# Two edits to a two-network float32 forward pass: attention statistics and head steps, and the recurrent mixer's taps, decays and padding units

## The chip, the core and the metric

The kernel runs on one core of one Trainium2 chip. The metric is the device time of one execution in microseconds. A core has TensorE (PE, matrix products into PSUM), VectorE (DVE), ScalarE (ACT), GpSimd (POOL) and SyncE (SP, which here only issues transfers). The engines run their own instruction streams in order and wait for one another on semaphores.

## The reference

The kernel computes two small networks in a row on 256 tokens with model width 1024, all in float32. Only the parts around the change are shown; feed-forward and convolution blocks stand between them.

```python
# first network, layer 0: 8 MLA heads and 8 forgetting ("fox") heads, 16 meta tokens in front
q = (rms_norm(c_q, g_cq) @ w_uq).reshape(b, l, MLA_HEADS, MLA_QK)
kv = (rms_norm(c_kv, g_ckv) @ w_ukv).reshape(b, l, MLA_HEADS, MLA_NOPE + MLA_V)
q = rope_tail(rms_norm(q, g_q_mla), cos, sin)
k = rope_tail(rms_norm(k, g_k_mla), cos, sin)
qf = rms_norm(fq.reshape(b, l, FOX_HEADS, FOX_DIM), g_q_fox)
kf = rms_norm(fk.reshape(b, l, FOX_HEADS, FOX_DIM), g_k_fox)
# both groups: blocked causal softmax attention (fox with cumulative log forget gates), then @ w_out

# second network, layer 1: the recurrent mixer
def mixer_b(h, w_in, conv_w, conv_b, w_a, b_a, w_x, b_x, lam, w_out):
    g, xb = jnp.split(h @ w_in, 2, axis=-1)
    g = jax.nn.gelu(g)
    xb = causal_dwconv(xb, conv_w, conv_b)          # 4 taps
    xh = xb.reshape(bsz, s, B_HEADS, B_HDIM)
    r = jax.nn.sigmoid(jnp.einsum("bshd,hde->bshe", xh, w_a) + b_a).reshape(bsz, s, B_WIDTH)
    i = jax.nn.sigmoid(jnp.einsum("bshd,hde->bshe", xh, w_x) + b_x).reshape(bsz, s, B_WIDTH)
    log_a = LRU_C * r * jax.nn.log_sigmoid(lam)
    a = jnp.exp(log_a)
    mult = jnp.sqrt(-jnp.expm1(2.0 * log_a))
    bterm = mult * (i * xb)
    _, hs = lax.associative_scan(_lin_rec_op, (a, bterm), axis=1)
    return (hs * g) @ w_out
```

## The kernel before

**Units.** Each float32 product is made of three products of float32r halves: weights hi with activations hi, weights hi with activations lo, weights lo with activations hi. The weights come in units of 8 (or 6) blocks of 128x128; a unit is 24 (or 18) matmuls on TensorE. SyncE fetches slabs of two units into `raw`, a ring of four slabs. For each unit ScalarE writes `whi` (`split_hi`, L361) and VectorE `wlo` (`split_lo`, L366), each into a ring of four. The splits run LA = 3 units ahead of the unit that the step works on: `ahead` in step j splits unit j+3, and `split_hi` waits until TensorE has left the unit four before.

**A phase's head.** The last steps of a phase split units 0, 1 and 2 of the next phase. Unit 3 is split in `act_root` and `dve_rstd`, ahead of the normalisation's root and reciprocal. That statistic is summed on GpSimd and multiplied out on TensorE (`pe_stats`, L447) after unit 1 of the new phase; ScalarE takes the root (L460) and VectorE the reciprocal (L467).

**Attention.** The first 18 units give tiles of 128 rows; ScalarE squares and copies the fox tiles, TensorE sums the squares by head (`fox_stats`), ScalarE and VectorE turn them into inverse norms, and `spread` (L911) spreads one over a pair of heads, into one of two PSUM banks that `fox_normed` (L1335) empties. The heads then run as a pipeline over 18 items (fox diagonal item, 8 fox heads, the first MLA head, the MLA diagonal item "D1" as item 10, 7 MLA heads). In step st TensorE does the scores of item st, the transposes (`turn`) of item st-2 and the values of item st-3; VectorE takes the maximum (`peak`) and the normalisation (`normal`), ScalarE the exponential (`exps`) and the copies (`turned`, `high`). The sums of squares of the MLA queries are products with 8 columns (`q_stats`, L952), seven for each of three parts, two passes each. `LATE` says in front of which steps the weights of the next phase are split.

**Recurrent mixer (`b_in`, 32 units, then `b_out`, 16 units of 6 blocks).** The order is written out by hand:

```python
B_ORDER = [("x", 0), ..., ("x", 5), ("r", 0), ("x", 6), ("x", 7), ("r", 1), ("x", 8), ("x", 9), ("r", 2),
           ("x", 10), ("x", 11), ("r", 3), ("g", 0), ("g", 1), ("g", 2), ("r", 4), ("g", 3), ("r", 5), ("g", 4)...]
```

An `x` unit gives one tile of the convolution's input, an `r` unit both gates of a pair of tiles, a `g` unit one gate tile. In step k VectorE splits unit k+3 (L366), scales tile k out of PSUM (L1611) and runs three taps of the tile before it (`taps`, L1597); behind an `r` step there is no tile waiting for its taps. GpSimd does the first tap with the bias (L2151) and, two steps behind, the lo half `hlo` (L2156) of what ScalarE wrote as `hhi` (L1954). It also multiplies the gate into the tile (L2147), squares the decays (L2138) and forms the scan's input (L2163). `r` unit f waits for `hlo` of tiles 2f and 2f+1. Tables such as `B_DECAY` and `B_MINUS` say in which step which tiles have their exponentials and tanh (L1960, L1962), the 1-a^2 (L1621), the root, the scan (L1626), the product with the gate (L1632) and the last halves (L1974, L1637). Units 30 and 31 of `b_in` are empty; of them one block is split, and TensorE skips them, adding 3 to `unit_done` at its last unit.

## Time and profile before

| | us |
|---|---|
| median of 3 runs | 1367.07 |
| lowest, highest of the three | 1361.7, 1375.7 |
| the profiled execution | 1372.0 |
| its span in the profile | 1370.3 |
| TensorE busy | 1333.2 (97%) |
| VectorE busy | 970.7 (71%) |
| ScalarE busy | 740.8 (54%) |
| GpSimd busy | 395.0 (29%) |

The page divides the span into 40 slices and gives the granted TensorE clock of each. The timeline gives for each group of instructions its start, its duration, and in brackets the idle time before it with what ended it. The windows view gives busy time by engine in a stretch.

### The profile page before, as it was taken

Reading aid. Unit: us, or ns where it says so; the run is one execution under the profiler, and the core shown is the slowest. Engines: PE = TensorE matmul, PEld = TensorE weight load, DVE = VectorE, ACT = ScalarE, POOL = GpSimd, SP = SyncE. Lnnn points to the kernel's source line nnn. Section 1 sums busy time; section 2 is a strip of 40 time slices with the busy share of each in tenths; the row PEclk is TensorE's granted clock in tenths of the full one; section 3 lists DMA queues with packets and bytes.
Section 4 is the critical chain, followed back from the end, with each engine's and each line's share of the span. In section 5 each row is a group of like instructions: output and inputs, shape, how many; then the busy total and the mean of one; then the engine's idle time right before and its main releaser. Section 6 shows DMA issues by size and latency. Waiting matters only on the chain. (4 is left out here: it accounts for less than half of the span.)

```text
span 1370.3 us, 28906 instructions
## 1 busy us (share of the span) xinstructions
PE 1333.2 (97%) x10820; PEld 1295.2 (95%) x10820; DVE 970.7 (71%) x1437; ACT 740.8 (54%) x1204; POOL 395.0 (29%) x406
## 2 busy tenths in 40 slices
PE   9999899999999999999999999999999899999996
PEld 8887599999999999999989999999999889999996
DVE  5856677665578777655655569998559798999854
ACT  5454655444444544444555547666455786766642
POOL 3621014320001233200445413333015541343310
PEclk9997999999999999999999999999999999999998
DMA  9430044555545555555544555554654445555451
GB/s 311 151 115 1 31 154 158 183 191 182 184 179 185 185 175 188 191 185 184 193 146 154 185 185 178 188 185 139 207 208 152 156 161 209 185 184 184 149 198 54
DMA packets 35372, 230.53 MB, mean 168 GB/s; under 512 B 4062, under 2 KB 5214, under 8 KB 11910
## 3 DMA queue, kind: packets, MB, share of 16 engines
q1 hardware_dynamic: 34228, 226.99, 47.6%
q10 hardware_dynamic: 1058, 2.38, 0.5%
q8 instruction: 56, 0.92, 0.3%
q14 instruction: 30, 0.25, 0.1%
HBM read 228.17 MB, written 1.05 MB: 167 GB/s over the span
## 5 line engine op out<-in xcount | busy, mean ns | idle before, releaser
L366 DVE TENSOR_TENSOR wlo<-raw,whi 128x1024 fp32r<-128x1024 f32 (+1 forms) x448 | 534.0, 1194 | 97.3 <-ACT whi L361 95.4
L403 PE MATMUL ps<-xhi,whi 128*128 128x256 f32 (+2 forms) x2048 | 579.7, 283 | 6.1 <-DVE wlo L366 5.4
L404 PE MATMUL ps<-xlo,whi 128*128 128x256 f32 (+2 forms) x2048 | 577.9, 282 | 0.0
L405 PE MATMUL ps<-xhi,wlo 128*128 128x256 f32 (+2 forms) x2048 | 576.8, 282 | 0.0
L361 ACT ACTIVATE whi<-raw 128x1024 fp32r<-128x1024 f32 (+2 forms) x446 | 447.7, 1007 | 153.3 <-PE ps L405 142.9
L403 PEld LDWEIGHTS ps<-xhi,whi 128*128 128x128 f32 x2048 | 386.5, 189 | 11.0 <-issue 7.6
L405 PEld LDWEIGHTS ps<-xhi,wlo 128*128 128x128 f32 x2048 | 387.1, 189 | 0.0
L404 PEld LDWEIGHTS ps<-xlo,whi 128*128 128x128 f32 x2048 | 384.8, 188 | 0.3
L403 PE MATMUL ps<-hhi,whi 128*128 128x256 f32 (+1 forms) x1184 | 334.8, 283 | 4.0 <-issue 2.7
L405 PE MATMUL ps<-hhi,wlo 128*128 128x256 f32 (+1 forms) x1184 | 333.9, 282 | 0.0
L404 PE MATMUL ps<-hlo,whi 128*128 128x256 f32 (+1 forms) x1184 | 333.7, 282 | 0.0
L403 PEld LDWEIGHTS ps<-hhi,whi 128*128 128x128 f32 x1184 | 224.3, 189 | 5.4 <-issue 3.0
L404 PEld LDWEIGHTS ps<-hlo,whi 128*128 128x128 f32 x1184 | 224.3, 189 | 0.0
L405 PEld LDWEIGHTS ps<-hhi,wlo 128*128 128x128 f32 x1184 | 224.1, 189 | 0.0
L510 POOL TENSOR_TENSOR ssum<-ssum,sq 128x256 f32<-128x256 f32 (+1 forms) x64 | 49.1, 767 | 448.0 <-ACT sq L491 448.0
L681 POOL TENSOR_TENSOR work<-work 128x256 f32<-128x256 f32 x48 | 66.1, 1378 | 175.6 <-ACT work L637 170.1
L528 DVE TENSOR_TENSOR h<-ps,h 128x256 f32<-128x256 f32 (+3 forms) x56 | 23.8, 424 | 117.3 <-PE ps L405 117.1
L652 ACT ACTIVATE work<-tmp,params 128x256 f32<-128x256 f32 x96 | 57.7, 601 | 87.0 <-DVE tmp L622 87.0
L595 POOL TENSOR_TENSOR hlo<-act,hhi 128x258 f32 (+1 forms) x64 | 66.7, 1042 | 119.4 <-ACT hhi L587 119.4
L479 ACT ACTIVATE xhi<-h,params 128x256 fp32r<-128x256 f32 (+1 forms) x56 | 28.6, 511 | 92.7 <-DVE h L528 85.5
L587 ACT ACTIVATE hhi<-act 128x258 fp32r<-128x258 f32 (+3 forms) x64 | 26.9, 420 | 88.1 <-DVE act L574 88.1
L613 DVE SCALAR_TENSOR_TENSOR work<-tmp,params,work 128x254 f32<-128x254 f32 x96 | 53.6, 558 | 10.4 <-DVE work L610 0.3
(287 smaller groups left out, 1312.4 us busy)
## 6 DMA issues: line engine op xcount, KB each, us to landing
raw<-w SPq DMA_DIRECT2D x182, 1024.0 KB, 4.8
raw<-w SPq DMA_DIRECT2D x40, 768.0 KB, 4.2
raw<-w SPq DMA_DIRECT2D x4, 512.0 KB, 5.3
h<-x_fm ACTq DMA_DIRECT2D x4, 272.0 KB, 5.6
out_fm<-h SPq DMA_DIRECT2D x8, 128.0 KB, 2.0
ws<-ws_src ACTq DMA_DIRECT2D x1, 512.0 KB, 3.7
bs<-bs_rows ACTq DMA_DIRECT2D x1, 512.0 KB, 6.6
consts<-constants SPq DMA_DIRECT2D x1, 508.0 KB, 12.0
```

The source lines that it names most:

```text
L361: nc.scalar.activation(whi[:, j % HLR, 0:n], raw[:, slot, col:col + n], ACT.Copy).then_inc(whi_done, 1)
L366: nc.vector.tensor_tensor(wlo[:, j % HLR, 0:n], raw[:, slot, col:col + n], whi[:, j % HLR, 0:n].bitcast(F32), ALU.subtract).then_inc(wlo_d ...
L403: nc.tensor.matmul(o, hi, xh, start=start, stop=False)
L404: nc.tensor.matmul(o, hi, xl, start=False, stop=False)
L405: mm = nc.tensor.matmul(o, lo, xh, start=False, stop=stop)
L479: nc.scalar.activation(xhi[:, kt, c0:c0 + t], h[:, kt, c0:c0 + t], ACT.Identity, scale=par(NORM_GAIN[n], kt)).then_inc(xhi_done, 1)
L510: nc.gpsimd.tensor_tensor(ssum[:, c0:c0 + t], ssum[:, c0:c0 + t], sq[:, slot, 0:t], ALU.add).then_inc(ssum_done, 1)
L587: nc.scalar.activation(hi[:, k, 0:t], src[:, j % 2, 0:t], ACT.Copy).then_inc(uhi_done, 1)
L595: nc.gpsimd.tensor_tensor(lo[:, k, 0:t], src[:, j % 2, 0:t], hi[:, k, 0:t].bitcast(F32), ALU.subtract).then_inc(ulo_done, 1)
L613: nc.vector.scalar_tensor_tensor(out=c[:, 2:SEQ], in0=x[:, 0:SEQ - 2], scalar=w0, in1=c[:, 2:SEQ], op0=ALU.mult, op1=ALU.add).then_inc(who ...
L652: nc.scalar.activation(cb[:, j % 4, :], tmp[:, j % 2, 0:SEQ], ACT.Identity, scale=par(f"f_conv_w{layer}", it * (3 * UB) + 3 * j + 2), bias ...
L681: nc.gpsimd.tensor_tensor(half[:, i % 2, :], gg[:, i % 2, :], cb[:, (2 * i + 1) % 4, :], ALU.mult).then_inc(u_done, 1)
```

## The change

**Attention.** The query statistics of the first two parts are split in two each, so five groups of 4, 3, 4, 3 and 7 products stand ahead of five transposes; GpSimd adds the halves (`q_part`). `spread` comes once behind each of eight units (8 to 15) where it came twice behind four; its lo half is made ahead of the weight split. The transposes of V go from behind units 14 and 15 to behind 16 and 17. The first transpose of item 0 goes one query tile later. D1's transpose and its copy come ahead of the scores and exponentials of item 12. The splits for the next phase go from in front of steps 11, 13, 15 to behind steps 13, 16, 18.

**Mixer.** The first tap moves from GpSimd to ScalarE. `B_DECAY` starts one step sooner, and the later tables move. The two empty units come first, so that the last two of the three units split during `f0_down` shrink to one block and the real units 1, 2 and 3 are split at the head of `b_in`.

```diff
+B_DECAY = {**steps(B_R3, (0, 1), (2, 3), (4, 5)), **steps(B_R5 + 4, (6, 7), (8, 9), (10, 11))}
+B_MINUS = {**steps(B_R3 + 3, 0, 2, 4), **steps(B_R5 + 6, 6, 8, 10)}
+B_ROOT = {**steps(B_R5, (0,), (3,)), **steps(B_R5 + 8, (6,), (9,))}
...
+B_LEAD = 2
+B_STEPS = len(B_ORDER) + KT
...
-            if p.name == "b_in" and it * UB + j + LA in (30, 31):
+            if last and p.next is ph["b_in"] and UB <= j + LA < UB + B_LEAD:
                 blocks = 1
...
-        LATE = {11: U_Q + 1, 13: U_Q + 2, 15: U_Q + 3}
+        LATE = {13: U_Q + 1, 16: U_Q + 2, 18: U_Q + 3}
+        D1 = items.index(("d", 1))
-        KEY_FINAL = {4: 0, 5: 1, 6: 2, 8: 3}
+        KEY_FINAL = {4: 0, 5: 1, 6: 2, 7: 3}
+        Q_PARTS = [(0, range(-1, 3)), (0, range(3, 6)), (1, range(-1, 3)), (1, range(3, 6)), (2, range(-1, 6))]
...
+                if 8 <= u < 16:
+                    spread(u // 12, u % 4, take_ring())
-                if u == 14:
+                if u == 16:
                     turn_v(1, (0, 1))
...
-                if j in (2, 3, 4):
-                    q_stats(j - 2)
+                if 1 <= j < 6:
+                    q_stats(j - 1)
...
-                if x == 5:
+                if x == 6:
                     turn(0)
-                if x == 6:
                     scores(3)
...
+                if st == D1 + 2:
+                    turn(D1)
                 if st < NIT:
                     scores(st)
...
-                        .then_inc(unit_done, 3 if k == len(B_ORDER) - 1 else 1)
+                        .then_inc(unit_done, 1 if k else 1 + B_LEAD)
...
             for st in range(4, NIT + 4):
+                step(st)
                 if st in LATE:
                     to(LATE[st])
-                step(st)
...
+            ahead_b(dve, split_lo, 1)
             for k in range(B_STEPS):
-                ahead_b(dve, split_lo, k)
+                ahead_b(dve, split_lo, k + B_LEAD)
...
                     act.wait_ge(s("q_stats_out"), 2)
+                    act.wait_ge(s("q_stats_sum"), 2)
...
+            act.wait_ge(wlo_done, p.unit0 + 1)
+            ahead_b(act, split_new, 1)
             for k in range(B_STEPS):
-                ahead_b(act, split_hi, k)
+                ahead_b(act, split_hi if k else split_new, k + B_LEAD)
...
+                if kind == "x":
+                    act.wait_ge(tile_free, p.tile0 + sum(x[0] != "r" for x in B_ORDER[:k + 1]))
+                    nc.scalar.activation(xb[:, f, :], tmp[:, f % 2, 0:SEQ], ACT.Identity, scale=par("b_conv_w", 4 * f + 3),
+                                         bias=par("b_conv_b", f)).then_inc(s("b_tap3"), 1)
                 if k >= 2 and k - 2 < len(B_ORDER) and B_ORDER[k - 2][0] == "x":
...
-                if kind == "x":
-                    pool.wait_ge(tile_free, tb + sum(x[0] != "r" for x in B_ORDER[:k + 1]))
-                    nc.gpsimd.tensor_scalar(xb[:, f, :], tmp[:, f % 2, 0:SEQ], par("b_conv_w", 4 * f + 3),
-                                            par("b_conv_b", f), ALU.mult, ALU.add).then_inc(s("b_tap3"), 1)
```

What TensorE does around the scores of item 4, in the change (the statistics are the rows with 128x8; the transposes follow them):

```order
L961 MATMUL ps<-consts,early 128x8 x4
L1124 MATMUL ps<-consts,wide 16x128 x2
L1126 MATMUL ps<-consts,wide 128x128 x3
L920 MATMUL ps<-inv,sel 128x272
L1095 MATMUL ps<-k_fox,q_fox 128x144
L1097 MATMUL ps<-consts 128x128
L1095 MATMUL ps<-k_fox,q_fox 128x272
L1097 MATMUL ps<-consts 128x128
L961 MATMUL ps<-consts,early 128x8 x3
```

The same piece of before, from the scores on:

```order
L1092 MATMUL ps<-consts 128x128
L952 MATMUL ps<-consts,early 128x8 x7
L1119 MATMUL ps<-consts,wide 16x128 x2
L1121 MATMUL ps<-consts,wide 128x128 x3
L1137 MATMUL ps<-extra,v_tok 64x258
```

Seven products in one place became four ahead of one transpose and three ahead of the next.

What VectorE does at the head of the mixer before, from the last tile of `f0_down` (add into `h`) to the first tile of the mixer:

```order
L366 TENSOR_TENSOR wlo<-raw,whi 128x1024 x2
L528 TENSOR_TENSOR h<-ps,h 128x256
L366 TENSOR_TENSOR wlo<-raw,whi 128x1024
L484 SCALAR_TENSOR_TENSOR xlo<-h,params,xhi 128x256
L366 TENSOR_TENSOR wlo<-raw,whi 128x1024
L467 RECIPROCAL rstd<-root 128x256
L1611 TENSOR_TENSOR tmp<-ps,rstd 128x256
```

And in the change:

```order
L373 TENSOR_TENSOR wlo<-raw,whi 128x128 x2
L535 TENSOR_TENSOR h<-ps,h 128x256
L373 TENSOR_TENSOR wlo<-raw,whi 128x1024
L491 SCALAR_TENSOR_TENSOR xlo<-h,params,xhi 128x256
L373 TENSOR_TENSOR wlo<-raw,whi 128x1024
L474 RECIPROCAL rstd<-root 128x256
L373 TENSOR_TENSOR wlo<-raw,whi 128x1024 x2
L1614 TENSOR_TENSOR tmp<-ps,rstd 128x256
```

Two full splits stood ahead of the add and now stand behind the reciprocal; the split behind the add is that of the first real unit, where it was that of the third.

What ScalarE does in three steps of the mixer, one behind an `r` step, before (`hhi` is L1954, the gates L1943 and L1948):

```order
L1954 ACTIVATE hhi<-work 128x256
L361 ACTIVATE whi<-raw 128x1024 x2
L1943 ACTIVATE work<-ps,params 128x256 x2
L1948 ACTIVATE act<-ps,params 128x256 x2
```

And in the change (L1961 is the first tap, L1966 `hhi`):

```order
L1961 ACTIVATE work<-tmp,params 128x256
L1966 ACTIVATE hhi<-work 128x256
L364 ACTIVATE whi<-raw 128x1024
L1961 ACTIVATE work<-tmp,params 128x256
L364 ACTIVATE whi<-raw 128x1024
L1951 ACTIVATE work<-ps,params 128x256 x2
L1956 ACTIVATE act<-ps,params 128x256 x2
```

The two weight splits stood back to back; now a first tap, which waits for VectorE's tile, stands ahead of each.

## Rows read from the trace of the kernel before

**Rows 1.** The page: TensorE's totals, and its clock in 40 slices

```profile
PE 1333.2 (97%) x10820; PEld 1295.2 (95%) x10820; DVE 970.7 (71%) x1437; ACT 740.8 (54%) x1204; POOL 395.0 (29%) x406
...
PEclk9997999999999999999999999999999999999998
```

**Rows 2.** TensorE's waits, whole span: total us, times, longest us

```profile
PE ps L1137 <- ACT extra L1750: 2.0, 1, 2.0
...
PE ps L911 <- DVE inv L1326: 1.8, 1, 1.8
...
PE ps L911 <- DVE k_fox L1335: 0.6, 1, 0.6
...
PE ps L1112 <- DVE wide L1393: 0.6, 1, 0.6
```

**Rows 3.** Windows: us, PE, PEld, DVE, ACT, POOL busy (x), clock, DMA share, GB/s

```profile
113.50:134.00 20.50, 20.50 (x78) 13.03 (x78) 8.42 (x30) 8.67 (x28) 0.00 (x0) 0.51 0.00 2
...
151.30:154.70 3.40, 3.40 (x16) 3.02 (x15) 2.41 (x7) 1.23 (x2) 0.00 (x0) 0.50 0.15 24
...
1017.60:1036.70 19.10, 17.73 (x147) 17.29 (x146) 15.29 (x21) 8.16 (x11) 6.15 (x7) 1.00 0.43 160
1036.70:1067.30 30.60, 29.01 (x240) 28.46 (x240) 29.84 (x39) 18.33 (x31) 16.61 (x16) 1.00 0.51 171
1067.30:1089.00 21.70, 17.82 (x144) 17.27 (x145) 15.14 (x19) 17.34 (x31) 9.74 (x9) 1.00 0.42 149
...
1112.50:1138.00 25.50, 21.88 (x166) 21.13 (x166) 23.82 (x30) 16.17 (x20) 8.64 (x6) 0.93 0.53 184
```

**Rows 4.** Timeline of TensorE in the head steps

```profile
112.07 1.73 PE L952 MATMUL ps<-consts,early 128*128 128x8 f32 x14
...
117.30 0.85 PE L1090 MATMUL ps<-k_fox,q_fox 104*128 104x144 f32 x2
...
124.52 0.85 PE L1090 MATMUL ps<-k_fox,q_fox 104*128 104x144 f32 x2
...
142.04 0.51 PE L1090 MATMUL ps<-k_mla,q_mla 96*128 96x144 f32 x2
...
145.31 0.51 PE L1090 MATMUL ps<-k_mla,q_mla 96*128 96x144 f32 x2
```

**Rows 5.** Timeline of ScalarE in the head steps

```profile
123.08 1.28 ACT L1703 ACT_TABLE_LOAD   x1
...
142.43 1.04 ACT L361 ACTIVATE whi<-raw 128x1024 fp32r<-128x1024 f32 x1
...
148.85 0.16 ACT L1756 ACTIVATE extra<-ps 16x16 f32<-16x16 f32 x1
```

**Rows 6.** Timeline of VectorE at the mixer's head and in its steps

```profile
1017.67 0.42 DVE L528 TENSOR_TENSOR h<-ps,h 128x256 f32<-128x256 f32 x1 [1.89 <-PE ps L405]
1018.01 1.22 DVE L366 TENSOR_TENSOR wlo<-raw,whi 128x1024 fp32r<-128x1024 f32 x1
...
1024.63 1.75 DVE L467 RECIPROCAL rstd<-root 128x256 f32<-128x256 f32 x1 [3.36 <-ACT root L460]
...
1028.43 1.55 DVE L1597 SCALAR_TENSOR_TENSOR work<-tmp,params,work 128x255 f32<-128x255 f32 x3
...
1050.68 2.17 DVE L1597 SCALAR_TENSOR_TENSOR work<-tmp,params,work 128x255 f32<-128x255 f32 x3
...
1053.90 2.90 DVE L1597 SCALAR_TENSOR_TENSOR work<-tmp,params,work 128x255 f32<-128x255 f32 x3
```

**Rows 7.** Timeline of ScalarE at the mixer's head

```profile
1024.12 0.47 ACT L460 ACTIVATE root<-ps,params 128x256 f32<-128x256 f32 x1 [2.93 <-PE ps L447]
...
1030.02 0.42 ACT L1954 ACTIVATE hhi<-work 128x256 fp32r<-128x256 f32 x1 [3.53 <-DVE work L1597]
1030.35 1.05 ACT L361 ACTIVATE whi<-raw 128x1024 fp32r<-128x1024 f32 x1
```

**Rows 8.** Timeline of TensorE where `b_out` begins

```profile
1115.71 0.36 PE L403 MATMUL ps<-hhi,whi 128*128 128x256 f32 x1 [2.65 <-issue]
```

More of the change, by code:

```diff
@@ L356, in split_hi @@
         def split_hi(act, rnd, j, blocks, first=False):
-            slot, col, n = (j // 2) % RAW, (j % 2) * blocks * P, blocks * P
+            slot, n = (j // 2) % RAW, blocks * P
+            col = (j % 2) * n
             act.wait_ge(raw_full[slot], rnd * 16 + 16)
@@ L361, in split_hi, with split_new @@
             nc.scalar.activation(whi[:, j % HLR, 0:n], raw[:, slot, col:col + n], ACT.Copy).then_inc(whi_done, 1)
+        def split_new(act, rnd, j, blocks):
+            split_hi(act, rnd, j, blocks, first=True)
         def split_lo(dve, rnd, j, blocks):
@@ L931, in k_stats, with q_stats @@
                 mm.then_inc(n_ss, 1)
-            def q_stats(k):
-                if k == 0:
-                    pe.wait_ge(q_eps_step, 6)
+            def q_stats(part):
+                k, xs = Q_PARTS[part]
+                pe.wait_ge(q_eps_step, 6 if k == 2 else 4)
                 m = META if k == 2 else P
-                for x in range(-1, 6):
-                    if k == 0 and x >= 0:
+                for x in xs:
+                    if x >= 0:
                         pe.wait_ge(n_sq[3], x + 1)
@@ L951, in q_stats @@
                         rhs = consts[:, K_QUAD + HEADS * Q_AT[x]:K_QUAD + HEADS * (Q_AT[x] + 1)]
-                    mm = nc.tensor.matmul(ps[0:m, 6, 2 * P + k * HEADS:2 * P + (k + 1) * HEADS], lhs, rhs, start=x < 0,
-                                          stop=x == 5)
+                    mm = nc.tensor.matmul(ps[0:m, 6, 2 * P + part * HEADS:2 * P + (part + 1) * HEADS], lhs, rhs,
+                                          start=x == xs[0], stop=x == xs[-1])
                 if k == 2:
@@ L999, in _ @@
                     fox_stats(u // 9)
-                if u in (8, 9):
-                    for i in (0, 1):
-                        spread(0, 2 * (u - 8) + i, take_ring())
-                if u in (12, 13):
-                    for i in (0, 1):
-                        spread(1, 2 * (u - 12) + i, take_ring())
-                if u == 14:
+                if 8 <= u < 16:
+                    spread(u // 12, u % 4, take_ring())
+                if u == 16:
                     turn_v(1, (0, 1))
-                if u == 15:
+                if u == 17:
                     turn_v(1, (2,))
@@ L1166, in _ @@
                     key_spread(KEY_SPREAD[st])
-                if st < NIT + 2:
+                if st < NIT + 2 and st != D1 + 2:
                     turn(st - 2)
@@ L1417, in _ @@
                     step(t - TL_Q - 4)
+                if t in (7, 11):
+                    inverse_lo(t // 11)
                 to(min(tile_unit[t], U_Q))
@@ L1421, in _ @@
                     inverse(0)
-                if t == 7:
-                    inverse_lo(0)
                 if t == 10:
                     inverse(1)
-                if t in (9, 10):
-                    for i in (0, 1):
-                        fox_normed(0, 2 * (t - 9) + i)
-                if t == 11:
-                    inverse_lo(1)
-                if t in (13, 14):
-                    for i in (0, 1):
-                        fox_normed(1, 2 * (t - 13) + i)
+                if 9 <= t < 13:
+                    fox_normed(0, t - 9)
+                if 13 <= t < 17:
+                    fox_normed(1, t - 13)
                 if t == 26:
@@ L1774, in step @@
             def step(st):
+                if st == D1 + 2:
+                    turned(D1)
                 if st < NIT:
                     exps(st)
-                if 2 <= st < NIT + 2:
+                if 2 <= st < NIT + 2 and st != D1 + 2:
                     turned(st - 2)
-                if st == 6:
+                if st == 7:
                     roots(3)
@@ L1792, in _ @@
                     roots(1)
-                if t == 15:
+                if t == 17:
                     turned_v(1, (0, 1))
-                if t == 16:
+                if t == 18:
                     turned_v(1, (2,))
@@ L1854, in _ @@
             for st in range(3, NIT + 3):
+                step(st)
                 if st in LATE:
                     to(LATE[st])
-                step(st)
             act.wait_ge(s("lam_exp_asked"), 1)
@@ L2081, in _ @@
             pool.wait_ge(qd_done, 2)
+            pool.wait_ge(s("q_stats_out"), 1)
+            for k in range(2):
+                nc.gpsimd.tensor_tensor(q_inv[:, k, :], q_part[:, 2 * k, :], q_part[:, 2 * k + 1, :],
+                                        ALU.add).then_inc(s("q_stats_sum"), 1)
             pool_residual(pool, ph["attn_out"], 1, 1, C1, T1)
@@ L2141, in _ @@
             for k in range(B_R5 + 11):
-                kind, f = B_ORDER[k] if k < 30 else (None, None)
                 before = B_ORDER[k - 1] if 0 < k <= 30 else (None, None)
```

40 lines of the change are left out of this document (18 added, 22 removed).

## The prediction

> **What bounds the kernel now.** I read the page first. TensorE is busy 97% of the span [rows 1], so no other engine's total matters; a change can only move TensorE's 37 us of idle time and the time it spends at the lower of its two clock levels. The reader should see in the clock row of the page that one slice stands out in the first tenth, and nothing else at this resolution. Then I took TensorE's waits in total: the largest single ones in attention are 2.0 us on ScalarE (`values`, L1137), 1.8 and 0.6 us at the spreads, and 0.6 us at the first transpose [rows 2]. The windows view then splits both touched places. In attention the stretch 113.5 to 134.0 has TensorE busy for all 20.5 us at a clock of 0.51, that is at 1.2 GHz nearly throughout, and 151.3 to 154.7 the same at 0.50; each of VectorE and ScalarE works under half of the first stretch [rows 3]. In the mixer TensorE idles 19.10 - 17.73 = 1.4, 1.6, 3.9 and 3.6 us in the four stretches shown [rows 3], and in the second one (ten units from the first `r` unit to the first `g` unit, 3.06 us each where a unit's own time is 2.9) VectorE is busy 29.84 of 30.6 us: there VectorE sets the pace.
>
> The profiled execution took 1372.0 us (span 1370.3), the three timed runs 1361.7, 1367.07 and 1375.7. The sum below is made against 1372.0. The profiled run stands 4.9 above the median, and the low-clock stretch alone is worth about 10 us, so I take it that the runs differ in how much of such stretches they hold; that is an inference, no row shows a second run.
>
> **Attention, the waits.** (a) The first spread waited 1.8 us because VectorE made the inverse's lo half behind a weight split; now it comes ahead of it, and VectorE had been idle there. The next ones waited 0.6 [rows 2] for `fox_normed`, which now has a whole unit (2.9 us) for each spread. VectorE does the same work in it, so I count -2.2 of 2.4. (b) The first transpose waited 0.6 for VectorE; one query tile later the operand is there: -0.5. (c) The 2.0 us at item 12: TensorE's `values` of the first MLA head needs the small copy of D1's probabilities, which ScalarE made at 148.85 behind two exponentials [rows 5]. In the change D1 comes first. But D1's transpose itself must follow the copies of item 9, and those ran late because a 1.04 us weight split stood at 142.43 in front of step 11 [rows 5]; that split moves too. About 0.5 us of wait stays, so -1.5. The splits now stand in front of steps 14, 17 and 19, each with the same small exposure as before. Sum of the waits: -4.2.
>
> **Attention, the clock.** The clock fell at the end of the second burst of fourteen passes of 8 columns, 1.73 us long [rows 4], and stayed low for 20.5 us. A head step took 124.52 - 117.30 = 7.2 us there against 145.31 - 142.04 = 3.3 us at full clock [rows 4]. The change makes five bursts (8, 6, 8, 6, 14 short passes), none over some 1.0 us beside more than 3 us of large products, except the last, whose weights have 16 columns. The work of the burst itself does not shrink. If the fall goes away, 20.5 us become 10.3: -10.2. What was covered comes out: ScalarE's table load of 1.28 us for the query roots, a second one back to the exponential [rows 5], and the new wait for GpSimd's two additions (no row has their size; between nothing and the 0.7 us that a wide one would be) sit in one step; at 3.3 us a step they delay the next exponential, and I take +1.0 (from 0 to 2.5). The second low stretch, 3.4 us, followed the 2.0 us wait of (c), so it goes with it: -1.7. Sum: -10.9.
>
> The Trainium skill (TensorE: Matmul & The Clock Gate, "Part 1: The HAM clock gate") says that idleness of the array throttles it and that sustained matmul activity releases it. The row of this trace does not fit that: the array was never recorded idle in those 20.5 us and the clock stayed low. By that rule alone the split bursts would change nothing, and the sum would lack its 9.2 us; this is the first rival.
>
> **Mixer, the head.** Before, the add of the last tile of `f0_down` at 1017.67 was followed by the split of real unit 2 at 1018.01 [rows 6], and TensorE went straight on with unit 0, split earlier. Now the split at that place is unit 0's own, so TensorE waits from 1017.6 to 1018.01 + 1.22 = 1019.2: +1.6. Unit 1 is split behind that, in time. Unit 2 is worse: it is now split behind the reciprocal. The root starts at 1024.12 when the statistic is there [rows 7], the reciprocal takes 1024.63 to 1026.38 [rows 6], and a split of 1.22 ends at 1027.6. TensorE would be free at 1024.1: +3.5. Before, nothing waited here. What is queued behind on VectorE (the split of unit 3, tile 0) is late by the same amount, so nothing gives it back.
>
> **Mixer, the first tap.** On GpSimd it took ScalarE out of the chain. Now ScalarE's step is: hi split, first tap (waits for VectorE's tile), `hhi`. VectorE's next split waits for ScalarE's next hi split. From the end of the tile to there is a tap (priced as `hhi`, 0.42), `hhi` 0.42 and a hi split 1.05 [rows 7], 1.9 us. Where VectorE has taps between (2.17 us, [rows 6]) this is covered. Behind an `r` step it has none: in steps x6, x8 and x10 VectorE stands for 1.9 us, three times: +5.6. Since VectorE sets the pace in just this stretch, TensorE gets all of it. Against it, VectorE's three taps took 1.55 us where GpSimd was idle, 2.17 and 2.90 us beside GpSimd's work [rows 6]. Without the first tap GpSimd still has `hlo` and the gate product there, so the 2.17 may become 1.9 and the 2.90 stays: -0.3 for each of three pairs, and 0.5 us of slack in the way: -1.4.
>
> The Trainium skill (SBUF — State Buffer, "Who interferes with whom") has it that a VectorE instruction with two SBUF inputs and a GpSimd instruction that reads SBUF exclude each other for a whole instruction. The rows agree in kind (1.55 against 2.17 and 2.90).
>
> **Mixer, decays and tail.** The decays a step sooner fill ScalarE's time before the `g` units; the stretch 1067.3 to 1089.0 has 3.9 us of waits [rows 3] and most were for ScalarE. But the whole phase arrives late and the hi split of `r4` now stands behind the first decays. I take -0.5 (0 to -3). At the end `b_out`'s first unit waited 2.65 us [rows 8], because two of the three units split ahead were empty; that wait goes, with the low clock behind it (0.93 over 25.5 us, 1.8 us [rows 3]). But the second half of `b_out` needs the chain of the last six tiles (decay, root, term, scan, halves), which already ended 0.9 us after TensorE asked. That chain gets only some 2 us shorter, since two fewer splits stand in it. So of 2.65 + 1.8 + 0.9 = 5.3 us I count -2.6.
>
> Mixer: 1.6 + 3.5 + 5.6 - 1.4 - 0.5 - 2.6 = +6.2.
>
> **The sum.** 1372.0 - 4.2 - 10.9 + 6.2 = 1363.1. Against the median of 1367.07 this is -0.3%; what a measurement of this kernel can tell from no change is about 1% (13.7 us), so within 1% means 1353.4 to 1380.7.
>
> **The rivals.** *Forecast (0.45):* the low stretch in attention goes, the mixer costs about 6 us; 1363.1, own range 1358 to 1368.
> *The clock falls all the same (0.20).* The products of 8 columns are the same number, and the head steps at half clock stayed at half clock without them. Then 9.2 us are not gained: 1372.3.
> *The mixer costs nothing (0.20).* If VectorE's taps all ran at 1.55 us once GpSimd is free of the first tap, each pair would save 0.6 + 1.35 = 1.95 us and pay for its 1.9 us gap, and with the 3 us from the decays the mixer would come to 6.2 - 4.4 - 2.5 = -0.7: 1356. For it: GpSimd's queue is shorter, so its other work lands elsewhere. Against it: the gate product lies in the same place.
> *No visible change (0.10):* the low-clock stretches were particular to the profiled run, and the median of before holds few: 1367.07 - 4.2 + 6.2 = 1369.
> *Slower (0.05).* The other side: the head's idle times of 1.6 and 3.5 us and the gaps in the `x` steps bring the clock down in the mixer, as 2.65 us of waiting did before `b_out` and 2.0 us in attention. A unit then takes 5.8 us where VectorE gives one every 3.6: +2.2 us a unit. A stretch as long as that in attention, 20.5 us, costs 3.5 units, 8 us; two of them, with the clock in attention unmended, 1372.3 + 16 = 1388. It decides from the second such stretch on; one alone leaves the time within 1%.
>
> **How the numbers follow.** The likeliest is 1363.1. The range must reach from the mixer that costs nothing (1356, less 2 for table loads that stay covered) to the clock that falls all the same (1372.3, plus 2): 1354 to 1374; outside are the slower case and the edges of the others. Faster by over 1% needs under 1353.4: the low edge of the third case together with all of attention's waits, 0.13. Slower by over 1%: 0.05. Within 1%: 0.82.
>
> **What would show it.** In the changed kernel: (1) the clock row of 110 to 135 us at full; head steps of 3.3 to 4.5 us, one longer beside the table loads. (2) No wait at the first spread, under 0.6 us at D1. (3) At the head of the mixer two waits of TensorE, one at its first real unit of about 1.6 us and one at its third, behind the statistic, of about 3.5 us. (4) VectorE idle for 1.9 us, ended by ScalarE's hi split, in three steps behind `r` units; the time from the first `r` to the first `g` unit grows from 30.6 to about 34 us. (5) No wait at `b_out`'s first unit, up to 2 us at its ninth. It would be wrong if ScalarE's hi split came in time in (4), if (3) were covered, or if the clock fell in a new place.

## The result and the profile after

The changed kernel took 1382.47 us (median of 4 runs, 1378.59 to 1388.42) where the kernel before took 1366.1 (median of 4, 1361.7 to 1375.7): a ratio of 1.0103, 95% interval [1.0063, 1.0142]. The forecast was 1363.1, in a range up to 1374. The change makes the kernel about 1% slower; the forecast had the sign wrong and missed by 19.4 us. Among the twelve runs of e3 in the table below, one of 1389.05 us counts as a slow run and is left out of its two means.

The page of the changed kernel, its execution of 1378.59 us (busy time of each engine, then the clock row), and its view of TensorE's waits (line, releaser: us in total, times, longest):

```profile
span 1376.9 us, 28912 instructions
PE 1333.5 (97%) x10820; PEld 1294.9 (94%) x10820; DVE 965.4 (70%) x1437; ACT 746.5 (54%) x1216; POOL 384.1 (28%) x396
PEclk9999899999999999999999999999999999999998
```
```profile
PE ps L410 <- DVE wlo L373: 10.9, 12, 3.7
PE ps L1124 <- DVE wide L1399: 4.0, 2, 2.6
PE ps L410 <- DVE hlo L1640: 3.2, 3, 2.2
PE ps L1259 <- DVE wlo L373: 2.9, 1, 2.9
```

TensorE's busy time is that of [rows 1] within 0.3 us. The waits on VectorE's lo splits (L373) are new, and so are the 4.0 us on `wide`, VectorE's scaled probabilities. The 1.8 us wait at the first spread and the 2.0 us wait of [rows 2] are gone; a wait of 0.54 us at a later spread and one of 0.53 us for D1's copy are left.

The windows view of the changed kernel, TensorE alone (stretch, its length, busy time, granted clock, DMA), and TensorE's timeline in the mixer (start, duration, line, and in brackets the idle time before it and its releaser):

```profile
110.00:134.00 24.00, 23.04 (x161) 1.00 0.01 1
134.00:156.00 22.00, 19.30 (x110) 1.00 0.00 1
156.00:160.00 4.00, 1.46 (x6) 0.75 0.65 211
160.00:168.00 8.00, 8.00 (x22) 0.50 0.07 27
168.00:172.00 4.00, 4.00 (x21) 0.55 0.02 4
1020.00:1030.00 10.00, 6.30 (x39) 0.83 0.37 131
```
```profile
1014.37 0.36 PE L410 MATMUL ps<-xhi,whi 128*128 128x256 f32 x1 [1.70 <-issue]
1024.39 0.36 PE L410 MATMUL ps<-xhi,whi 128*128 128x256 f32 x1 [3.70 <-DVE wlo L373]
...
1050.92 0.36 PE L410 MATMUL ps<-xhi,whi 128*128 128x256 f32 x1 [1.58 <-DVE wlo L373]
...
1061.61 0.35 PE L410 MATMUL ps<-xhi,whi 128*128 128x256 f32 x1 [1.02 <-DVE wlo L373]
...
1072.30 0.36 PE L410 MATMUL ps<-xhi,whi 128*128 128x256 f32 x1 [1.02 <-DVE wlo L373]
...
1084.88 0.39 PE L1259 MATMUL ps<-hhi,whi 128*128 128x256 f32 x1 [2.87 <-DVE wlo L373]
...
1123.29 0.38 PE L410 MATMUL ps<-hhi,whi 128*128 128x256 f32 x1 [2.22 <-DVE hlo L1640]
```

The stretch that ran at 0.51 before [rows 3] is at full clock now, but a new one, 158.0 to 171.6 us, runs at 1.2 GHz (0.50); it begins in the last half microsecond of a 2.60 us wait, which ends at 158.54. The start of `attn_out` comes at 168.4 us instead of 174.5, a gain of 6.1 where 15.1 were forecast; the mixer takes 10.9 us more where 6.2 were forecast.

**How the runs are compared.** Each run has its span and its mean granted clock. Span times clock is about what the same work and waits would take at full clock; the rest of the span is lost to the lower level. (It is approximate where VectorE sets the pace.) The two parts behave differently: in 35 runs of the kernel before, time at full clock was 1354.1 with a standard deviation of 2.3, while the loss went from 6.8 to 30.3 us, mean 12.1. In the profiled run of before, on which the forecast's sum was made, the loss was 17.8. The last two columns are means over the runs. Their standard errors are 0.2 to 0.8 us for time at full clock and 0.8 to 1.9 for the loss (2.3 for the changed kernel, which has four runs). The before in brackets ran beside that kernel on the same chip. e1 to e4 are from one chip, e5 to e8 from a second, e9 to e12 from a third and e13 from a fourth, so kernels of different groups are best compared by their difference from their own before.

| kernel | median us | ratio, 95% | at full clock (before) | low-clock loss (before) |
|---|---|---|---|---|
| changed kernel | 1382.5 | 1.0103 [1.0063, 1.0142] | 1363.0 (no clock on record) | 18.3 |
| e1 attention edits | 1369.7 | 1.0012 [0.9987, 1.0038] | 1353.3 (1354.1) | 15.5 (12.1) |
| e2 mixer edits | 1378.1 | 1.0069 [1.0044, 1.0095] | 1361.5 (1354.1) | 15.5 (12.1) |
| e3 lead and decays | 1370.1 | 1.0011 [0.9981, 1.0042] | 1354.0 (1354.1) | 15.1 (12.1) |
| e4 first tap | 1375.7 | 1.0048 [1.0020, 1.0076] | 1360.4 (1354.1) | 13.5 (12.1) |
| e5 e1, late splits back | 1365.0 | 0.9992 [0.9972, 1.0012] | 1351.9 (1354.5) | 12.1 (11.0) |
| e6 e1, lo halves later | 1360.0 | 0.9949 [0.9926, 0.9973] | 1351.0 (1354.5) | 7.9 (11.0) |
| e7 tap a step later | 1365.6 | 0.9989 [0.9959, 1.0018] | 1350.3 (1354.5) | 14.2 (11.0) |
| e8 query parts | 1367.4 | 1.0002 [0.9983, 1.0022] | 1355.2 (1354.5) | 10.6 (11.0) |
| e9 e6 and e7 | 1357.2 | 0.9935 [0.9911, 0.9959] | 1347.4 (1353.8) | 8.7 (11.1) |
| e10 changed, both mends | 1359.9 | 0.9966 [0.9946, 0.9987] | 1349.6 (1353.8) | 10.1 (11.1) |
| e11 e10, head mended | 1358.9 | 0.9940 [0.9920, 0.9961] | 1349.5 (1353.8) | 8.0 (11.1) |
| e12 decays | 1364.4 | 0.9989 [0.9966, 1.0012] | 1351.9 (1353.8) | 12.2 (11.1) |
| e13 e10 without lead | 1357.8 | 0.9928 [0.9902, 0.9954] | 1346.8 (1354.4) | 10.4 (12.8) |

### The profile page after: what moved, and what is told of

Read it like the earlier page. It is cut to its first block and busy times, and to the rows that moved or that the text cites. A ratio compares the mean times of both kernels' runs of the same rounds, so it can differ in the third digit from the quotient of the medians.

```text
span 1376.9 us, 28912 instructions
## 1 busy us (share of the span) xinstructions
PE 1333.5 (97%) x10820; PEld 1294.9 (94%) x10820; DVE 965.4 (70%) x1437; ACT 746.5 (54%) x1216; POOL 384.1 (28%) x396
## 5 line engine op out<-in xcount | busy, mean ns | idle before, releaser
L373 DVE TENSOR_TENSOR wlo<-raw,whi 128x1024 fp32r<-128x1024 f32 (+2 forms) x448 | 532.6, 1191 | 110.0 <-ACT whi L364 107.9
L410 PE MATMUL ps<-xhi,whi 128*128 128x256 f32 (+2 forms) x2048 | 580.7, 284 | 13.7 <-DVE wlo L373 10.9
L620 DVE SCALAR_TENSOR_TENSOR work<-tmp,params,work 128x254 f32<-128x254 f32 x96 | 53.6, 558 | 10.4 <-DVE work L617 0.3
```

What stands on the lines that cost most here:

```text
L373: nc.vector.tensor_tensor(wlo[:, j % HLR, 0:n], raw[:, slot, col:col + n], whi[:, j % HLR, 0:n].bitcast(F32), ALU.subtract).then_inc(wlo_d ...
L410: nc.tensor.matmul(o, hi, xh, start=start, stop=False)
L620: nc.vector.scalar_tensor_tensor(out=c[:, 2:SEQ], in0=x[:, 0:SEQ - 2], scalar=w0, in1=c[:, 2:SEQ], op0=ALU.mult, op1=ALU.add).then_inc(who ...
```

## The experiments

### The change in four pieces: e1, e2, e3, e4

e1 is the kernel before with the hunks of the change in attention, e2 with those in the mixer, e3 with the mixer's tables, the lead and its bookkeeping but the first tap left on GpSimd, and e4 with nothing but the tap:

```diff
 # e4, ScalarE, step k; GpSimd loses the same tap
+                if kind == "x":
+                    act.wait_ge(tile_free, ...)
+                    nc.scalar.activation(xb[:, f, :], tmp[:, f % 2, 0:SEQ], ACT.Identity, scale=..., bias=...)
```

> The attention edits alone; the mixer is as before. Theory A (the low-clock stretch only moves, its cause is a wait of VectorE and ScalarE behind a late weight split): the segment to the start of attn_out takes about 168.4 us as in the changed kernel (174.5 before), the profile shows a stretch of 10 to 15 us at about 0.50 after a wait of 2 us or more behind steps 14 to 17, and span times mean clock, the time that the same work would take at full clock, is 1352 (1352.5 before). The time is then 0 to 6 us under before. Theory B (my forecast's: the low stretch is gone for good, and the changed kernel lost it again elsewhere): a median 10 to 15 us under before (ratio 0.990) and no low-clock stretch in attention.

> The mixer edits alone (lead of two empty units, first tap on ScalarE, decays a step sooner); attention as before. Theory A (the mixer carries the loss): mixer from its first unit to the end of its output phase 9 to 11 us longer, about 7.5 of it in waits (head 1.6 and 3.7, three gaps of 1.9 less 0.5 of slack, 2.9 at r4, less 2.7 at b_out) and the rest in dips of the clock; span times mean clock about 1360; time 9 to 14 us over before, ratio 1.008. Theory B (my forecast's size): +6 us, ratio 1.004.

> The mixer edits without the first tap, which stays on GpSimd; attention as before. If the lead costs by itself: waits of 1.6 and 3.7 us at the head, no wait at the first unit of b_out, and 1036.7 to 1067.3 stays 30.6 us. The 2.9 us at r4 is disputed: it stays if the decays in front of ScalarE's hi split make it (theory A, then +5 us, span times clock 1357), and goes if the late first tap makes it (theory B, then +2.5 us, 1355).

> The first tap on ScalarE alone; all else as before. Theory A (split, tap, split follow one another between ScalarE and VectorE): VectorE stands 1.9 us in front of three weight splits behind r units, first r to first g unit 34.5 us instead of 30.6, span times clock 1356.5, time +4 us. Theory B (relief of VectorE's taps pays for it): first r to first g unit 30.6 to 32 us, time within 1.5 us of before.

Measured at full clock: attention -0.8, mixer +7.4, lead with decays -0.1, tap +6.3. Attention with its -0.8 is theory A's 1352 within the error; its loss to the low level is 3.4 us above that of before, with a standard error of 1.2. For the mixer theory A (1360) is nearer than the forecast's size. e3, at 1354.0, lies under both of its theories (1357 and 1355). The tap's own cost is most of the mixer's, and more than either theory of e4 had; VectorE's lo splits in e4, from its timeline, and ScalarE around the first 1.93 us gap in the changed kernel:

```profile
1045.73 2.16 DVE L366 TENSOR_TENSOR wlo<-raw,whi 128x1024 fp32r<-128x1024 f32 x1 [1.48 <-ACT whi L361]
1050.16 1.22 DVE L366 TENSOR_TENSOR wlo<-raw,whi 128x1024 fp32r<-128x1024 f32 x1 [1.93 <-ACT whi L361]
1053.34 1.23 DVE L366 TENSOR_TENSOR wlo<-raw,whi 128x1024 fp32r<-128x1024 f32 x1 [0.19 <-ACT whi L361]
1056.29 2.31 DVE L366 TENSOR_TENSOR wlo<-raw,whi 128x1024 fp32r<-128x1024 f32 x1
1060.86 1.23 DVE L366 TENSOR_TENSOR wlo<-raw,whi 128x1024 fp32r<-128x1024 f32 x1 [1.93 <-ACT whi L361]
```
```profile
1051.14 0.60 ACT L1961 ACTIVATE work<-tmp,params 128x256 f32<-128x256 f32 x1 [2.57 <-DVE tmp L1614]
1051.64 0.40 ACT L1966 ACTIVATE hhi<-work 128x256 fp32r<-128x256 f32 x1
1051.95 1.04 ACT L364 ACTIVATE whi<-raw 128x1024 fp32r<-128x1024 f32 x1
```

ScalarE waits for VectorE's tile, runs tap (0.60), `hhi` (0.40) and hi split (1.04), and only then may VectorE split: 1.93 us, as forecast, three times (the third in e4 is at 1071.56). The forecast's list has three such gaps; the first row shows a fourth, of 1.48 us, behind the first `r` unit. The rows of 2.16 and 2.31 show that splits of 1.22 us are now stretched beside GpSimd's work (four in e4; in the changed kernel three: 2.17, 2.31, 2.31). Over the stretch from the first `r` unit to `r4` VectorE's taps take 14.1 us in e4 where they took 22.3, its lo splits 20.1 where they took 15.8, and in front of those it stands idle for 9.3 us where it stood for none. So the relief came, 3 us of busy time in all, and the gaps were larger than forecast.

In e4 TensorE's wait for GpSimd at the first `r` unit is 2.85 us where it was 1.28 (L1253 waits in the two timelines), and the stretch from the first `r` unit to `r4` grew from 39.8 to 45.2 us (up to the first `g` unit from 30.6 to 34.6, as sign (4) of the prediction had it). Together 7.0; the mean is 6.3.

The 2.9 us at `r4`, disputed between the theories of e3, is 1.32 us there; with the late tap it is 2.87. So both make it: 0.9 of it the decays' (0.44 before), and 1.5 more comes with the tap. Alone, in e4, the tap takes the wait only from 0.44 to 0.84.

### Attention: the late splits, e5 and e6

e5 puts the three splits back into their old places; e6 leaves ScalarE's hi halves where the change has them and moves only VectorE's lo halves:

```diff
 # e5
-        LATE = {13: U_Q + 1, 16: U_Q + 2, 18: U_Q + 3}
+        LATE = {10: U_Q + 1, 12: U_Q + 2, 14: U_Q + 3}
 # e6, VectorE alone
                 step(st)
-                if st in LATE:
-                    to(LATE[st])
+                if st - 1 in LATE:
+                    to(LATE[st - 1])
```

> The attention edits with the three late weight splits back in their old places (in front of steps 11, 13 and 15). Theory A (the late splits make the waits of 1.4 and 2.6 us, and the 2.6 us wait brings the clock down): both waits shrink under 1 us or move in front, no low stretch at 160 to 172; the part of the time lost to low clock (span times one minus mean clock) falls from 15.5 to about 10, time 5 us under that of the attention edits alone (1364 to 1366). Theory B (the clock falls near the end of attention whatever stands there): loss stays at 15, time stays at 1370.

> The attention edits, with VectorE's lo half of each of the three late splits one step later than ScalarE's hi half, so that the next step's products of VectorE do not stand behind it. Theory A (ScalarE idle for 2.06 us in front of its next exponential comes from VectorE's lo split standing in front of VectorE's work for that step): that idle time falls to about 1 us, TensorE's waits of 1.4 and 2.6 us lose about 1 us each, span times mean clock 1351.5, and the low stretch at 160 to 172 goes or gets shorter. Theory B (the hi half of 1.05 us alone makes the wait): no change, 1353.3 and 15.5.

VectorE's timeline in e1, then in e6, around the second late split (`soft` holds the maxima and sums of a head's scores; ScalarE's exponential waits for it):

```profile
155.57 1.23 DVE L367 TENSOR_TENSOR wlo<-raw,whi 128x1024 fp32r<-128x1024 f32 x1 [2.39 <-ACT whi L362]
156.71 0.65 DVE L1374 TENSOR_REDUCE soft<-ps 128x1 f32<-128x144 f32 x2
157.39 0.16 DVE L1381 TENSOR_TENSOR soft<-soft,q_neg 128x2 f32<-128x2 f32 x1
...
158.95 0.56 DVE L1393 TENSOR_SCALAR wide<-wide,soft 128x144 f32<-128x144 f32 x2
```
```profile
152.92 0.66 DVE L1374 TENSOR_REDUCE soft<-ps 128x1 f32<-128x144 f32 x2 [1.41 <-PE ps L1091]
...
153.88 0.56 DVE L1393 TENSOR_SCALAR wide<-wide,soft 128x144 f32<-128x144 f32 x2
...
154.94 1.23 DVE L367 TENSOR_TENSOR wlo<-raw,whi 128x1024 fp32r<-128x1024 f32 x1
```

In e1 VectorE stands for 2.39 us in front of a split whose hi half ScalarE makes behind a whole head step, and the next head's maxima stand behind the split. ScalarE's exponential is late by that (2.06 us of idle time), the second `wide` of the step comes at 158.95, and TensorE's transposes of it wait 2.61 us. In e6 the maxima come first, and ScalarE's idle time in front of its exponentials there is 0.90 and 1.16 us. The exposure itself is old: in before, ScalarE's idle time behind its three late splits was 2.18, 2.17 and 2.06 us. But TensorE had more work queued at those places. Its windows from 134 to 172 us, in before, e1 and e6:

```profile
134.00:172.00 38.00, 33.79 (x199) 0.95 0.08 28
```
```profile
134.00:172.00 38.00, 32.74 (x159) 0.82 0.08 29
```
```profile
134.00:172.00 38.00, 35.80 (x232) 1.00 0.17 56
```

TensorE is idle for 4.2, 5.3 and 2.2 us. The windows of e1 and of e6 (here with all engines; the clock is the third number from the end):

```profile
160.00:168.00 8.00, 8.00 (x26) 4.01 (x25) 2.43 (x5) 3.69 (x10) 0.00 (x0) 0.57 0.15 63
168.00:172.00 4.00, 4.00 (x23) 4.00 (x22) 3.18 (x18) 1.16 (x2) 0.00 (x0) 0.59 0.00 0
```
```profile
160.00:168.00 8.00, 8.00 (x62) 7.28 (x62) 6.02 (x23) 3.13 (x7) 0.62 (x1) 1.00 0.06 26
168.00:172.00 4.00, 4.00 (x36) 4.00 (x35) 4.00 (x6) 3.04 (x7) 0.88 (x3) 1.00 0.80 264
```

The low stretch behind the wait is in the profiles of the changed kernel and of e1, which have that wait, and in none of e5, e6, e9, e10, e11 and e13, which have the attention edits without it. In means, each against its own before: time at full clock is -0.8 in e1 and -3.5 in e6, 2.7 less, and the loss is +3.4 in e1 and -3.1 in e6, 6.5 less; both are four standard errors. Theory A of e6 holds: ScalarE's idle time falls to about 1 us and the waits of 1.42 and 2.61 us are gone. For e5 theory A's time came (1365.0), but its fall in loss against e1 is 2.3 us by the same reckoning, one and a half standard errors, so e5 alone does not show it. The edit is two lines that move three instructions by a step, and it makes the attention half worth -0.5% (e6) where it was worth nothing. e5 lies between: its waits are a 1.8 us one for D1's copy and a 0.9 us one on `wide`, the first followed by a low stretch of 3.4 us, and its loss is that of before within the error.

The Trainium skill (TensorE: Matmul & The Clock Gate, "Part 1: The HAM clock gate") says that idleness throttles the array. For this stretch the runs agree with it: the clock fell at 2.6 us of waiting, and not where the wait was taken away. The idleness does not account for what comes next, since the clock then stays low for 10.2 us in e1 and 13.6 us in the changed kernel while TensorE is recorded busy, as it did for the 20.5 us of [rows 3] without a wait ahead.

### The bursts of short products: e8

> Kernel before with only the query statistics in five parts instead of three (with GpSimd's additions and the roots a step later that belong to it); spreads, splits and D1 as before. Theory A (the bursts of fourteen short passes bring the clock down at 113 us): full clock from 113 to 134, the loss to low clock falls from a mean of 12.1 by 3 to 6 us, since the stretch at this place was 20, 19, 5 and 5 us long in four profiles with the old bursts. Theory B (the bursts don't matter, the waits at the spreads ahead of them do): low stretches at 113 in this profile too and a mean loss of 11 to 13.

```diff
 # e8: the kernel before with this, its GpSimd additions, and the roots one step later
-                if j in (2, 3, 4):
-                    q_stats(j - 2)
+                if 1 <= j < 6:
+                    q_stats(j - 1)
```

The profile of e8 has full clock from 112 to 140 us, but it is low from 145 to 152 us, behind D1's 2.0 us wait, and again from 162.5 to 166. (A wait of 4.2 us at its first spread ends at 45 us; the clock falls at 43, inside it, for 6.8 us.) The mean loss is 10.6 us against 11.0, and the time is that of before (ratio 1.0002). So theory B fits the means and theory A the one profile. Over all profiles: with the three long bursts the clock fell between 108 and 136 us in before, e2, e3, e4 and e12 (for 20, 20, 7, 7 and 7 us) and not in e7; with the five parts it did not in the changed kernel, e1, e5, e8, e9, e10 and e13, and did in e6 (3 us) and e11 (some 14 us). So the fall is rarer where the five parts are, 2 of 9 profiles against 5 of 6. But eight of those nine kernels also have the other attention edits, only e8 has the parts alone, and its mean loss is 0.4 us under that of before with an error of 1.3: that the parts make the fall rarer is not shown. That stretch was thus never a fixed 20.5 us of the kernel before.

### The tap a step later: e7, and both mends: e9

```diff
 # ScalarE, step k, behind the hi split of this step
-                if kind == "x":
-                    act.wait_ge(tile_free, ... B_ORDER[:k + 1] ...)
-                    nc.scalar.activation(xb[:, f, :], tmp[:, f % 2, 0:SEQ], ...)
+                if 1 <= k <= 30 and B_ORDER[k - 1][0] == "x":
+                    g = B_ORDER[k - 1][1]
+                    act.wait_ge(tile_free, ... B_ORDER[:k] ...)
+                    nc.scalar.activation(xb[:, g, :], tmp[:, g % 2, 0:SEQ], ...)
```

> Kernel before with the first tap on ScalarE, but one step later, behind the hi half of the next step's split. Theory A (the cost of the tap on ScalarE is the order split, tap, split between two engines): the three gaps of 1.9 us of VectorE in front of splits go, first r to first g unit 29 to 31 us instead of 34.5, span times mean clock 1354 or less (1360.4 with the tap a step sooner). Theory B (ScalarE's added work is the cost, wherever it stands): 1358 to 1361.

> Attention edits with the lo halves a step later, and the mixer of before with the first tap on ScalarE one step later; no lead, decays as before. Theory A (the two gains add): span times mean clock 1351.0 - 4.2 = 1346.8, loss to low clock about 8 to 10, time 1355 to 1358, ratio 0.992. Theory B (they share their cover, or the shorter waits bring the clock down elsewhere): ratio 0.995 or more, no better than the attention half alone.

VectorE in e7, one round of the same stretch (x3 are a tile's three taps):

```profile
1045.94 1.51 DVE L1597 SCALAR_TENSOR_TENSOR work<-tmp,params,work 128x255 f32<-128x255 f32 x3
1047.36 1.22 DVE L366 TENSOR_TENSOR wlo<-raw,whi 128x1024 fp32r<-128x1024 f32 x1
1048.50 2.96 DVE L1597 SCALAR_TENSOR_TENSOR work<-tmp,params,work 128x255 f32<-128x255 f32 x3
1051.38 1.22 DVE L366 TENSOR_TENSOR wlo<-raw,whi 128x1024 fp32r<-128x1024 f32 x1
```

In the round shown no gap is left in front of the splits; the round before it has one of 0.66 us. One group of taps per round has become 1.51 us where it was 2.17 [rows 6]; the other stays at 2.96 (2.90 before). The stretch from the first `r` unit to `r4` takes 38.1 us (before 39.8, e4 45.2), and the wait for GpSimd at the first `r` unit is gone. At full clock e7 is at -4.2 where e4 is at +6.3: 10.5 us between two places of one instruction per tile. Theory A holds: not ScalarE's extra work but the order is the cost. e9 has both mends, and they add up within the error of about 1 us: -3.5 - 4.2 = -7.7 were to come by the two runs, -7.0 by the value expected, -6.4 came.

The Trainium skill (SBUF — State Buffer, "Who interferes with whom") has a VectorE instruction with two inputs in SBUF contend with a GpSimd instruction that reads SBUF. The rows agree: with the tap off GpSimd, one group of taps runs at 1.51, and the one beside the gate product (GpSimd's, 1049.2 to 1050.7) at 2.96. In e4 the gate product lies at 1056.05, beside the lo split that took 2.31.

### What is left of the change when it is mended: e10 to e13

e10 is the changed kernel with the edits of e6 and e7. e11 also has, at the head of the mixer:

```diff
 # e11, VectorE; on ScalarE the hi half likewise ahead of act_root
-            dve_rstd(dve, 6, META, SEQ, ph["b_in"])
-            ...
-            ahead_b(dve, split_lo, 1)
+            split_ahead(dve, split_lo, p, 0, 0, False)
+            ahead_b(dve, split_lo, 1)
+            dve_rstd(dve, 6, META, SEQ)
```

e12 is the kernel before with `B_DECAY`'s first three steps one sooner and nothing else. e13 is e9 with e12's line, that is e10 without the lead and the later tables that belong to it.

> The changed kernel as given, with two mends of order: VectorE's lo halves of the late splits in attention one step later, the first tap on ScalarE one step later. Theory A (the loss is the two orders; lead and decays net nothing): as the run without lead and decays beside it, 1346.8 at full clock, ratio 0.992. Theory B (the lead costs its 5.3 us of head waits once the rest is mended, since the decays' relief is then had twice): 1349 to 1352, ratio 0.995.

> As the run before it, and at the head of the mixer the split of the third real unit stands ahead of the norm's root on ScalarE and of its reciprocal on VectorE. Theory A (that order made the 3.7 us wait at the third unit): the wait goes under 0.7 us, the 1.7 us at the first unit stays, span times mean clock 3 us under the run before. Theory B (the reciprocal is what the next unit's tiles need, so its delay by a split of 1.2 us costs as much later): within 1 us of the run before.

> Kernel before with nothing but the first three pairs of decays one step sooner. My forecast's size: -0.5 us at full clock (0 to -3). Theory A (they take away the waits of 1.8 and 1.6 us between the first g unit and r5 and add 0.9 at r4): -2.5 us, 1352. Theory B (the wait only moves): within 0.7 us of 1354.3.

> The mended change (lo halves in attention and first tap each a step later, decays a step sooner) without the lead of two empty units. Theory A (the terms add: the lead costs about 2 us): span times mean clock 1347.4 - 1.9 = 1345.5, time about 1355, ratio 0.992. Theory B (tap and decays share their gain, the lead is free): 1347.4 to 1349.6 at full clock, as the two runs beside which it stands.

TensorE at the head of the mixer in e10 and in e11:

```profile
1006.21 0.36 PE L410 MATMUL ps<-xhi,whi 128*128 128x256 f32 x1 [1.70 <-issue]
...
1016.22 0.55 PE L410 MATMUL ps<-xhi,whi 128*128 128x256 f32 x1 [3.71 <-DVE wlo L373]
```
```profile
1011.20 0.36 PE L410 MATMUL ps<-xhi,whi 128*128 128x256 f32 x1 [1.70 <-issue]
...
1021.22 0.35 PE L410 MATMUL ps<-xhi,whi 128*128 128x256 f32 x1 [0.88 <-DVE wlo L373]
```

In e10 the third unit waits 3.71 us. In e11 it does not wait; the row of 0.88 us there is the fourth unit, so theory A's wait did go. Yet the time is the same (-0.1 at full clock). The traces say where the 2.8 us went: e10 goes from the first `r` unit to `r4` in 36.9 us without a wait of TensorE over 0.4 us, e11 takes 39.3 and waits 0.81 and 1.12 us in it, and e13, which has no head waits, takes 39.4. VectorE sets the pace there, and a wait of TensorE ahead of such a stretch lets VectorE run ahead by as much; taken away, it comes back inside. Theory B of e11 holds in its number. Its reason, the later reciprocal, is another way to say that VectorE's work and not TensorE's wait sets when the `r` units come; no run tells the two apart.

The decays alone are worth -1.9 at full clock, between the forecast's -0.5 and theory A's -2.5: the waits of 1.81 and 1.58 us between the first `g` unit and `r5` (they are in the idle time of 1067.3 to 1089.0 in [rows 3]) go, 0.9 comes at `r4`, and new waits of 0.89 and 0.71 us stand ahead of `b_out`. From the first `r` unit to `b_out` e12's profile takes 77.8 us where before took 79.0. e10 (1349.6) falls on theory B's side: with the rest mended, the lead costs. Its size is the difference of e10 and e13: 1349.6 - 1346.8 = 2.8 us, or 3.4 if each is set against its own before, since the two ran on different chips; the standard error is 0.6 to 0.9. e13's 1346.8 lies between its theories (1345.5, and 1347.4 or more) and does not part them, but e10 against e13 says that the lead is not free, as theory B has it. In the traces the lead's two head waits are 5.4 us, the pace gives back 2.4 of them, and the 2.7 us at `b_out` go while 2.2 come at its ninth unit: 2.5 net, near the 2.8.

e9 (1357.2) and e13 (1357.8) are the best kernels, 0.7% under before and 1.8% under the changed one. The decays' -1.9 does not show in the medians of the two.

## Why the prediction was wrong

The forecast was 19.4 us low. By the two measures of the table 7.5 of it lie in time at full clock (forecast 1372.0 - 1.7 - 17.8 - 3.2 + 6.2 = 1355.5, measured 1363.0) and 12.4 in the loss (forecast 17.8 - 11.9 = 5.9, measured 18.3); they sum to 19.9, half a microsecond of which is mean against median. The 7.5 are 4.0 in attention (e1 has 1353.3 where the sum has 1352.5 - 3.2 = 1349.3; 1.6 of it because the profiled run stood 1.6 under the mean), 1.2 in the mixer (e2's +7.4 for +6.2), and 2.3 that the changed kernel has above the sum of e1 and e2.

**The step that failed first: "If the fall goes away, 20.5 us become 10.3: -10.2".** The stretch did go away, as (1) foresaw, but the term set it against the one profiled run. Over 35 runs the loss of before has a mean of 12.1 us, not 17.8, and profiles of kernels with the same attention have a stretch of 0 to 20 us at that place. At most the mean can be gained. The prediction took note that the profiled run stood above the median and that low stretches may be the reason; it drew a rival of 0.10 from it and not the sum. By size this is the smaller failure: e6, which has all of the attention edits without the new wait, loses 7.9 us where the forecast had 5.9. Against its own before that is a gain of 3.1 and not of 11.9.

**The second: "The splits now stand in front of steps 14, 17 and 19, each with the same small exposure as before".** ScalarE's exposure was indeed the same, 2.06 and 2.05 us behind the first two (no exponential follows the third). But I priced it by what TensorE had felt of it at the old places and did not ask what TensorE has queued at the new ones. There it felt 1.42 and 2.60 us. So the waits' -4.2 with +1.0 came to -0.8 in all, and with the 2.60 us wait the clock fell for 13.6 us. e6 shows it: 2.7 us at full clock and 6.5 us of loss go when the lo half is moved, 9.2 of the 19.4. This is the largest single part of the miss. That the clock could fall "in a new place" stood in the prediction's last line, without a price.

**D1, the spreads, the transpose** went as the steps said: no wait at the first spread, 0.53 us at D1. **The head** too: 1.70 and 3.70 us for 1.6 and 3.5. But "nothing gives it back" was wrong, as e11 shows. **The gaps** were 1.93 us, three of them, as forecast. **The relief of -1.4** came as well, 3 us of VectorE's busy time with the stretched splits already taken off; what the term left out was a fourth gap of 1.48 us, smaller ones of 0.2 to 0.5, and the GpSimd wait at the first `r` unit, which grew by 1.6: the tap measured +6.3 for +4.2. **Decays** -1.9 for -0.5, **lead with decays** -0.1 for +2.0. So the mixer's sum, 6.2, is near e2's +7.4 by luck: its pieces were off by 2 us each, in opposite ways. e1 and e2 add to +6.6 at full clock, the changed kernel has +8.9; the 2.3 between, with only four runs of the changed kernel, whose chip is not on record, stay open.

**The tail** came as (5) said: no wait at `b_out`'s first unit, 2.22 at its ninth. But its term of -2.6 did not: 2.65 - 2.22 is 0.4, and the 3.4 us dip that followed the first wait (at 1117 us) follows the second one (at 1124).

**Rivals.** "The clock falls all the same" was nearest in kind, though it put the fall at the old place. "Slower" named the head's idle time as what brings the clock down; the profile has a dip of 3.4 us there (0.83 over 1020 to 1030) and one behind the 2.87 us wait at `r4`, worth 1.7 us each, and not its 20 us stretches. e2, e3 and e4 each have such dips, and their losses, 15.5, 15.1 and 13.5 against 12.1, are each within about two standard errors of it.

## What to carry to other kernels

When two engines hand a buffer back and forth (hi half on one, lo half on the other), put the second engine's half behind its next urgent work, and put new work of the first behind the next half it owes: two such moves by one step were worth 10.5 us here and 2.7 us, the second with 6.5 us of low-clock loss besides. Take a gain in clock from the mean loss over many runs, never from the length of a low stretch in one profile, and price the largest wait that the change makes with the clock that may follow it. Ahead of a stretch that another engine paces, a wait of TensorE can be given back inside it, as 2.4 of 2.8 us were in e11: price it by the pace of that stretch and not by its own length.

## What the hardware did that I had not expected

With a wait of 2.60 us came 13.6 us at 1.2 GHz with TensorE busy after it, while one of 3.70 us at the mixer's head was followed by a dip of only 3.4 us (0.83 over 10 us): how long the lower level holds is not set by the length of the wait. Whether the clock falls does go with the wait. The fifteen profiles hold 32 waits of TensorE of 2.0 us or more, and at 30 of them the clock fell, inside the wait or within some 2 us behind it (the other two are the waits of 2.7 us at `b_out` in e4 and e9); of the 30 waits of 1.4 to 2.0 us elsewhere than at the kernel's end, 6. Only the two waits of 2.6 us ahead of the last head steps were followed by more than 6.8 us. The 20.5, 20.5 and 13.6 us stretches near 113 us in before, e2 and e11 have no such wait ahead, and their cause stays open. Every profile also ends with 8 to 12 us at the lower level, 4 to 6 us of each loss, which none of the edits touches. The same kernel lost from 6.8 to 30.3 us to the lower level in 35 runs, which is nearly the whole of its spread in time. And of what VectorE's taps gained when work left GpSimd (8.2 us over the stretch in e4), half was taken back by lo splits (2.31 for 1.22), which now lay beside GpSimd's gate product.
